# Eleven norm borders of a transformer stack: sums with one column of ones, and other places for sums, spreads and pieces

## The chip, the cores and the metric

The kernel runs as one program on one core of one Trainium2 chip. The metric is the device time of a run in microseconds (us). The five engines are TensorE (PE in the profile, PEld for its weight loads), VectorE (DVE), ScalarE (ACT), GpSimd (POOL) and SyncE (SP); they run side by side and wait for one another through semaphores.

## The reference, cut to what matters

The reference is a stack of four layers (differential attention, a gated linear recurrence, a sliding-window attention with sinks, differential attention again) followed by a second block (retention, a gated linear recurrent unit and a convolutional feed-forward), for 512 tokens of 1024 features in float32. The change touches only the norms between the parts:

```python
def layer_norm(x, g, b):
    mu = jnp.mean(x32, axis=-1, keepdims=True)
    var = jnp.mean(jnp.square(x32 - mu), axis=-1, keepdims=True)
    y = (x32 - mu) * lax.rsqrt(var + LN_EPS) * g.astype(jnp.float32) + b.astype(jnp.float32)
...
def rms_norm_2(x, w):
    y = x32 * lax.rsqrt(jnp.mean(x32 * x32, axis=-1, keepdims=True) + RMS_EPS)
...
        h = layer_norm(ALPHA * h + y, ln_g[i, 0], ln_b[i, 0])
        u = jnp.square(jax.nn.relu(h @ w_up[i])) @ w_down[i]
        h = layer_norm(ALPHA * h + u, ln_g[i, 1], ln_b[i, 1])
```

There are eight layer norms (numbered 0 to 7 here, even ones after a mixer, odd ones after a feed-forward) and three root-mean-square norms (8 to 10).

## The kernel before, in words

**Data.** Activations lie features-first: `h` is 128 partitions by 8 feature chunks by 512 tokens. Every big product is split into three float32r passes (high weight by high activation, high by low, low by high), so that each product of one weight block and one chunk is three matmuls (L472 to L474 over all 512 tokens, L571 to L573 over 256). Weights come as slabs of 1 MB through a ring of SBUF slots; GpSimd makes the high part of a slab (L451), VectorE the low part (L1637). A "unit" is what TensorE does with one slab: 8 chunks k = 0 to 7 of the contraction, two output blocks, results in two of the four PSUM banks `proj`. The other four banks are `mix`.

**A norm border.** The last two units ahead of a norm and the first two behind it are worked in halves of 256 tokens, so that the norm of one half lies under the matmuls of the other. The function `pair` writes TensorE's order by hand: first the first halves of both units, then the second halves, (ua, hf 0), (ub, hf 0), (ua, hf 1), (ub, hf 1), each of 8 chunks of 6 matmuls. A dictionary `points` says before which chunk two short jobs are put in:

- `stats(l, hf)` sums over the features: matmuls with the sums over chunks (`s1` of h, `s2` of its squares, 128x128 blocks) as weights and a tile of ones as the moving operand, 8 matmuls for a layer norm (16 instructions of the trace, since a float32 matmul is two passes), 4 for a root-mean-square norm.
- `spread(l, hf)` brings the two scalars of each token back along the free dimension (transposes of a broadcast column, L560).

A pair that produces the norm's input is called with `made=l` and holds stats and spread of half 0; the pair behind it is called with `read=l` and holds those of half 1. In the reading pair TensorE also waits before each chunk of half 0 for that chunk's low part, made by GpSimd at L446 (`half_x`, one semaphore step for each of five pieces: k = 0, k = 1, k = 2 and 3, k = 4 and 5, k = 6 and 7). At odd norms no pair follows: TensorE runs the four short units of the "ple" product (each 12 matmuls of 512 columns), with stats of half 1 behind the first and spread of half 1 behind the second, and then whole units that read the normalised values.

**VectorE at a border** (`border`) works strictly in its written order: add the product to h for half 0 and sum (`half`, `sums`, L1726 or L1728, L1743), the scalars of half 0 (`norm_scalars`, L1752 to L1765), `half(2, 1)` (which waits for the end of TensorE's unit ua), `apply(0, 0)` and `apply(0, 1)` (multiply and subtract for pieces 0 to 2 and 3 to 4 of half 0, L1777 and L1779), `sums(l, 2, 1)`, `half(3, 1)`, `sums(l, 3, 1)`, then the scalars and the applying of half 1. **ScalarE** squares (L1095), takes the square root (L1104), and for each piece writes the scaled value rounded (`xh`, L1112) and in full (`h`, L1115), in its own written order; GpSimd's L446 follows the latter. At odd norms ScalarE also copies the ple products out (L1414).

Of the kernel before, what the change touches and what calls it, by code (L numbers as in the profile page):

```python
# [21 lines left out]
ALU = mybir.AluOpType  # L22
ACT = mybir.ActivationFunctionType

P = 128
S = 512
D = 1024
# [4 lines left out]
RMS_EPS = 1e-6  # L32
# [178 lines left out]
def build(nc, stream, xin, pin, pos, vecs, relb, onehot, eye, swap, picks, decay, out):  # L211
    with ExitStack() as ctx:
# [255 lines left out]
        def _(pe):  # L468
# [71 lines left out]
            def stats(l, hf):  # L540

                for q, total, sem_ in ((0, s1, M("s1_added")), (1, s2, M("s2_added"))):
                    if q == 0 and l >= 2 * NL:
                        continue
                    pe.wait_ge(sem_, 5 * l + (5 if hf else 3))
                    for t in range(2 * hf, 2 * hf + 2):
                        for part in range(2):
                            at = (2 * q + t % 2) * P
                            last = nc.tensor.matmul(mix[:, 0, at:at + P], total[:, part, t * P:(t + 1) * P], ones[:, :],  # L549
                                                    start=part == 0, stop=part == 1, skip_group_check=True)  # L550
                last.then_inc(M("stats"), 1)

# [23 lines left out]
            def pair(ua, which, gen, made=None, read=None):  # L576

                ub = ua + 1
                points = {}
                if made is not None:  # L580
                    points[(ua, 1, 6 if made == 8 else 4)] = (stats, made, 0)
                    points[(ub, 1, 1) if made == 8 else (ua, 1, 7)] = (spread, made, 0)
                if read is not None:
                    points[(ub, 0, 1) if read == 8 else (ua, 0, 6)] = (stats, read, 1)
                    points[(ub, 0, 6 if read == 8 else 0)] = (spread, read, 1)
                for u, hf in ((ua, 0), (ub, 0), (ua, 1), (ub, 1)):
                    if hf == 0:
                        begin_unit(u)
                    for k in range(8):
                        if (u, hf, k) in points:  # L590
                            do, l, half = points[(u, hf, k)]
                            do(l, half)
                        if read is not None and hf == 0:
                            if read < 2 * NL:
                                pe.wait_ge(M("half_x"), 5 * read + PIECE_OF[k] + 1)
                            else:
                                pe.wait_ge(M("half_r"), 8 * (read - 8) + k + 1)
                        elif gen is not None:
                            operand_wait(which, gen, k)
                        last = half_chunk(u, k, hf, X if which == "x" else G, made is not None)  # L600
                    if hf:
                        last.then_inc(unit_done, 1)
                    elif made is not None:
                        last.then_inc(M("half_done"), 1)
# [436 lines left out]
        def _(act):  # L1041
# [64 lines left out]
            def ln_pieces(l, hf, pieces):  # L1106

                for p in pieces:
                    k0, n = PIECES[p]
                    act.wait_ge(M("ln_u"), 10 * l + 5 * hf + p + 1)  # L1110
                    for k in range(k0, k0 + n):
                        A(xh[:, k, cols(hf)], h[:, k, cols(hf)], ACT.Identity, scale=col("ln_g", 8 * l + k), bias=col("ln_b", 8 * l + k))\  # L1112
                            .then_inc(*own.sig(xh_ready if hf and k % 2 else None))
                    for k in range(k0, k0 + n):
                        A(h[:, k, cols(hf)], h[:, k, cols(hf)], ACT.Identity, scale=col("ln_g", 8 * l + k), bias=col("ln_b", 8 * l + k))\  # L1115
                            .then_inc(*own.sig(M("ln_full") if k == k0 + n - 1 else None))
# [260 lines left out]
            for layer in range(NL):  # L1377
                if layer % 3 == 0:
                    da_mixer(layer // 3, layer)
                elif layer == 1:  # L1380
                    hg_mixer(layer)
                else:
                    sw_mixer(layer)
                squares(2 * layer, 0)
                act.dma_start(pf[:, :, :], pin[layer]).then_inc(M("p_in"), 16)
                squares(2 * layer, 1)
                warm(ACT.Sqrt)
                squares(2 * layer, 2, 0)
                squares(2 * layer, 3, 0)
                std(2 * layer, 0)  # L1390
                squares(2 * layer, 2, 1)
                ln_pieces(2 * layer, 0, range(4))
                squares(2 * layer, 3, 1)
                ln_pieces(2 * layer, 0, (4,))
                std(2 * layer, 1)
                ln_pieces(2 * layer, 1, range(5))
                act.wait_ge(M("p_in"), 16 * (layer + 1))
                A(ph[:, :, :], pf[:, :, :], ACT.Copy).then_inc(*own.sig(M("p_hi")))
                ffn(layer)
                l = 2 * layer + 1  # L1400
                squares(l, 0)
                squares(l, 1)
                warm(ACT.Sqrt)
                squares(l, 2, 0)
                squares(l, 3, 0)
                std(l, 0)
                squares(l, 2, 1)
                ln_pieces(l, 0, range(3))
                squares(l, 3, 1)
                s0, u0 = PLAN.at[f"ple{layer}"]  # L1410

                def ple(j):
                    done(u0 + j)
                    A(po[:, 2 * j:2 * j + 2, :], banks(u0 + j), ACT.Copy).then_inc(*own.sig(rel["act"]))  # L1414

                ln_pieces(l, 0, (3,))
                ple(0)
                ln_pieces(l, 0, (4,))
                std(l, 1)
                ple(1)  # L1420
                ln_pieces(l, 1, (0, 1))
                ple(2)
                ln_pieces(l, 1, (2, 3))
                ple(3)
                ln_pieces(l, 1, (4,))
                s0, u0 = PLAN.at[f"gate{layer}"]
                for j in range(4 if layer < NL - 1 else 2):
                    done(u0 + j)
                    if j >= 2:
                        act.wait_ge(M("h_new"), layer * 4 + j - 1)  # L1430
                    A(sg[:, j % 2], banks(u0 + j), ACT.Sigmoid).then_inc(*own.sig(rel["act"]))
                    p2 = slice(2 * j, 2 * j + 2)
                    if layer < NL - 1:
                        act.wait_ge(M("h_new"), layer * 4 + j + 1)
                        A(gh[:, p2, :], h[:, p2, :], ACT.Copy).then_inc(*own.sig(gh_ready))
                    else:
                        squares(8, j)
# [179 lines left out]
        def _(dve):  # L1617
# [127 lines left out]
            def norm_scalars(l, hf):  # L1745

                c = 2 * hf
                m, v, r, mr = (small[:, a + c:a + c + 2] for a in (200, 204, 208, 212))
                total, squared = mix[:, 0, 0:2 * P:P], mix[:, 0, 2 * P:4 * P:P]
                dve.wait_ge(M("stats"), 2 * l + hf + 1)  # L1750
                if l < 2 * NL:
                    V.tensor_scalar(m, total, 1.0 / D, None, ALU.mult).then_inc(*own.sig())  # L1752
                    mine()
                    V.scalar_tensor_tensor(v, m, -1.0, m, ALU.mult, ALU.mult).then_inc(*own.sig())
                    mine()
                    V.scalar_tensor_tensor(v, squared, 1.0 / D, v, ALU.mult, ALU.add).then_inc(*own.sig())
                    mine()
                    V.tensor_scalar(v, v, 0.0, LN_EPS, ALU.max, ALU.add).then_inc(*own.sig(M("var_done")))
                else:
                    V.tensor_scalar(v, squared, 1.0 / D, RMS_EPS, ALU.mult, ALU.add).then_inc(*own.sig(M("var_done")))  # L1760
                dve.wait_ge(M("std_done"), 2 * l + hf + 1)
                V.reciprocal(r, v).then_inc(*own.sig(M("norm_ready") if l >= 2 * NL else None))
                if l < 2 * NL:
                    mine()
                    V.tensor_tensor(mr, m, r, ALU.mult).then_inc(*own.sig(M("norm_ready")))  # L1765
# [42 lines left out]
            def border(l, scaled, apply):  # L1808
# [21 lines left out]
                half(2, 1)  # L1830
                apply(0, 0)
                sums(l, 2, 1)
                if l % 2 == 0 or l > 8:
                    apply(0, 1)
                half(3, 1)
                sums(l, 3, 1)
                if l % 2 and l < 8:
                    apply(0, 1)
                norm_scalars(l, 1)
                apply(1, 0)  # L1840
                apply(1, 1)
# [655 lines left out]
```

## Time and profile before

| | |
|---|---|
| time, median of 3 runs | 3677.19 us (3676.24 to 3681.41) |
| profiled execution, its own time | 3681.41 us |
| its span | 3679.6 us |
| granted TensorE clock over the span | 0.989 |
| TensorE busy | 3565.8 us, 97% |
| VectorE, ScalarE, GpSimd busy | 1826.0, 941.3, 828.9 us |

The profile comes from one execution; it is the slowest of the three runs, 4.2 us over the median. Starts in a timeline are microseconds from the start of the span. A matmul's duration in a row includes its way through the array, so that rows of a dense stream overlap; the step from one start to the next is its cost.

### The profile page before, as it was taken

To read this page: it belongs to the slowest core of one execution; us is meant where nothing else is said; L and a number is where in the kernel's file an instruction comes from. 1 tells how busy PE (TensorE), PEld (TensorE's weight loads), DVE (VectorE), ACT (ScalarE), POOL (GpSimd) and SP (SyncE) were. 2 spreads that over 40 slices of the span, in tenths; PEclk is the share of its full clock that TensorE was granted. 3 is DMA by queue.
4 is the path that set the end of the run, shared out by engine and by line. 5 is a ranking of instruction groups with operands and counts; after the bars stand their busy time and mean duration, and the time that the engine had idled before them with its cause. 6 is when DMAs were issued, how large, how long until landed. Compare 5 with 4: busy or idle time off the path is not lost.

```text
span 3679.6 us, 44420 instructions
## 1 busy us (share of the span) xinstructions
PE 3565.8 (97%) x18618; PEld 2997.9 (81%) x18618; DVE 1826.0 (50%) x2281; ACT 941.3 (26%) x1662; POOL 828.9 (23%) x374
## 2 busy tenths in 40 slices
PE   8989999999999999999999998999989999999998
PEld 6778888798888888678888877888888887788887
DVE  5555334635563336564335555543464445563434
ACT  2552001312230013540113255210141214120102
POOL 2113222311032223122223211322221111222221
PEclk9999999999999999999999999999999999999999
DMA  5312222221122222222222321222212222222222
GB/s 201 103 58 92 92 103 81 93 78 60 56 89 92 100 95 92 72 75 92 94 101 81 109 81 58 95 92 102 82 69 92 81 92 79 94 103 92 103 92 69
DMA packets 57279, 329.58 MB, mean 90 GB/s; under 512 B 5579, under 2 KB 12235, under 8 KB 20348
## 3 DMA queue, kind: packets, MB, share of 16 engines
q1 hardware_dynamic: 44604, 303.79, 23.2%
q10 hardware_dynamic: 12480, 22.96, 1.9%
q8 instruction: 151, 2.47, 0.3%
q14 instruction: 44, 0.36, 0.0%
HBM read 323.96 MB, written 8.80 MB: 90 GB/s over the span
## 4 chain that ended last, share of the span: by engine, by line
PE 86%; DVE 8%; ACT 4%; issue 1%; POOL 1%; DMA 1%; DVEq 0%; ACTq 0%
PE proj L472 23%; PE proj L474 23%; PE proj L473 23%; PE proj L571 2%; PE proj L573 2%; PE proj L572 2%; DVE s L1743 2%; PE proj L505 2%; PE proj L507 1%; PE proj L506 1%; PE mix L738 1%; PE mix L644 1%; DVE wlo L1637 1%; PE mix L549 1%; PE mix L670 1%
## 5 line engine op out<-in xcount | busy, mean ns | idle before, releaser
L451 POOL TENSOR_SCALAR whi<-raw 128x2048 fp32r<-128x2048 f32 x286 | 729.0, 2549 | 2573.8 <-DMA raw<-in_stream 2573.8
L472 PE MATMUL proj<-gh,whi 128*128 128x512 f32 x1968 | 786.4, 400 | 14.7 <-DVE wlo L1643 10.6
L474 PE MATMUL proj<-gh,wlo 128*128 128x512 f32 x1968 | 771.4, 392 | 0.0
L473 PE MATMUL proj<-gl,whi 128*128 128x512 f32 x1968 | 770.9, 392 | 0.0
L1637 DVE TENSOR_TENSOR wlo<-raw,whi 128x2048 fp32r<-128x2048 f32 x286 | 700.0, 2450 | 126.6 <-POOL whi L451 114.9
L472 PE MATMUL proj<-xh,whi 128*128 128x512 f32 x1760 | 698.0, 397 | 14.9 <-DVE wlo L1637 5.8
L473 PE MATMUL proj<-xl,whi 128*128 128x512 f32 x1760 | 691.2, 393 | 0.0
L474 PE MATMUL proj<-xh,wlo 128*128 128x512 f32 x1760 | 691.1, 393 | 0.0
L472 PEld LDWEIGHTS proj<-gh,whi 128*128 128x128 f32 x1968 | 371.2, 189 | 108.3 <-issue 15.8
L474 PEld LDWEIGHTS proj<-gh,wlo 128*128 128x128 f32 x1968 | 371.0, 189 | 81.1
L473 PEld LDWEIGHTS proj<-gl,whi 128*128 128x128 f32 x1968 | 371.4, 189 | 79.2 <-issue 2.2
L472 PEld LDWEIGHTS proj<-xh,whi 128*128 128x128 f32 x1760 | 332.3, 189 | 95.1 <-issue 10.1
L474 PEld LDWEIGHTS proj<-xh,wlo 128*128 128x128 f32 x1760 | 332.6, 189 | 72.8
L473 PEld LDWEIGHTS proj<-xl,whi 128*128 128x128 f32 x1760 | 332.8, 189 | 71.8 <-issue 1.4
L1373 ACT ACTIVATE rl<-proj 128x1024 f32<-128x1024 f32 x64 | 65.7, 1027 | 946.8 <-PE proj L474 934.6
L1728 DVE TENSOR_TENSOR h<-h,proj 128x1024 f32<-128x1024 f32 (+1 forms) x76 | 80.0, 1053 | 350.8 <-PE proj L474 329.7
L2123 DVE SCALAR_TENSOR_TENSOR hid<-proj,rl 128x1024 f32<-128x1024 f32 x64 | 78.4, 1224 | 313.4 <-ACT rl L1373 312.5
L571 PE MATMUL proj<-xh,whi 128*128 128x256 f32 x640 | 184.5, 288 | 15.5 <-POOL xl L446 15.5
L572 PE MATMUL proj<-xl,whi 128*128 128x256 f32 x640 | 181.7, 284 | 0.0
L573 PE MATMUL proj<-xh,wlo 128*128 128x256 f32 x640 | 181.7, 284 | 0.0
L505 PE MATMUL proj<-whi,gh 128*128 128x256 f32 x512 | 152.1, 297 | 0.0
L506 PE MATMUL proj<-wlo,gh 128*128 128x256 f32 x512 | 145.8, 285 | 0.0
(295 smaller groups left out, 4331.5 us busy)
## 6 DMA issues: line engine op xcount, KB each, us to landing
raw<-in_stream SPq DMA_DIRECT2D x286, 1024.0 KB, 4.8
da_b<-bias_da ACTq DMA_DIRECT2D x16, 512.0 KB, 3.4
bias_da<-bias_rows ACTq DMA_DIRECT2D x8, 512.0 KB, 9.3
h<-in_x ACTq DMA_DIRECT2D x4, 512.0 KB, 8.7
bias_sw<-bias_table ACTq DMA_DIRECT2D x1, 2048.0 KB, 10.4
pf<-in_p ACTq DMA_DIRECT2D x4, 512.0 KB, 5.5
sw_b<-bias_sw ACTq DMA_DIRECT2D x4, 512.0 KB, 3.4
out_features<-fin SPq DMA_DIRECT2D x8, 256.0 KB, 2.3
```

Of the source, the lines that this page charges most:

```text
L451: nc.gpsimd.tensor_scalar(whi[SLOT[n]][:, :, :], raw[SLOT[n]][:, :, :], 1.0, 0.0, ALU.mult, ALU.add).then_inc(hi_done, 1)
L472: nc.tensor.matmul(out, wh, ah, start=first, stop=False, skip_group_check=check)
L473: nc.tensor.matmul(out, wh, al, start=False, stop=False, skip_group_check=check)
L474: return nc.tensor.matmul(out, wl, ah, start=False, stop=last, skip_group_check=check)
L505: nc.tensor.matmul(o, ah, wh, start=k == 0 and st % per == 0, stop=False, skip_group_check=True)
L506: nc.tensor.matmul(o, ah, wl, start=False, stop=False, skip_group_check=True)
L571: nc.tensor.matmul(o, wh, ah, start=k == 0 and (j if own_banks else hf) == 0, stop=False, skip_group_check=True)
L572: nc.tensor.matmul(o, wh, al, start=False, stop=False, skip_group_check=True)
L573: last = nc.tensor.matmul(o, wl, ah, start=False, stop=k == 7, skip_group_check=True)
L1637: V.tensor_tensor(wlo[SLOT[n]][:, :, :], raw[SLOT[n]][:, :, :], whi[SLOT[n]][:, :, :].bitcast(F32), ALU.subtract).then_inc(*own.sig(split_ ...
L1728: ins = V.tensor_tensor(o, o, y, ALU.add)
L2123: V.scalar_tensor_tensor(hid[:, :, :], banks(u), 0.0, rl[:, :, :], ALU.max, ALU.mult).then_inc(*own.sig(rel["dve"]))
```

## The change

The sums use one column of ones instead of 128, and write to one column for each token block (columns 0 to 3 the sums, 4 to 7 the sums of squares). The points move: stats of half 1 from before chunk 6 to before chunk 4 of (ua, hf 0) of the reading pair (not at norm 8); spread of half 0 from before chunk 7 of (ua, hf 1) to before chunk 0 of (ub, hf 1) of the producing pair (at norm 8 from chunk 1 to chunk 2 of (ub, hf 1)). ScalarE does all five pieces of half 0 before it squares the last pair of chunks of half 1, at all eight layer norms. VectorE does `apply(0, 1)` before `half(3, 1)` at norms 1, 3, 5 and 7 too, as it did at the others.

```diff
-                            at = (2 * q + t % 2) * P
-                            last = nc.tensor.matmul(mix[:, 0, at:at + P], total[:, part, t * P:(t + 1) * P], ones[:, :],
+                            last = nc.tensor.matmul(mix[:, 0, 4 * q + t:4 * q + t + 1], total[:, part, t * P:(t + 1) * P], ones[:, 0:1],
...
-                    points[(ub, 1, 1) if made == 8 else (ua, 1, 7)] = (spread, made, 0)
+                    points[(ub, 1, 2 if made == 8 else 0)] = (spread, made, 0)
                 if read is not None:
-                    points[(ub, 0, 1) if read == 8 else (ua, 0, 6)] = (stats, read, 1)
+                    points[(ub, 0, 1) if read == 8 else (ua, 0, 4)] = (stats, read, 1)
...
                 squares(2 * layer, 2, 1)
-                ln_pieces(2 * layer, 0, range(4))
+                ln_pieces(2 * layer, 0, range(5))
                 squares(2 * layer, 3, 1)
-                ln_pieces(2 * layer, 0, (4,))
                 std(2 * layer, 1)
...
                 squares(l, 2, 1)
-                ln_pieces(l, 0, range(3))
+                ln_pieces(l, 0, range(5))
                 squares(l, 3, 1)
...
-                ln_pieces(l, 0, (3,))
                 ple(0)
-                ln_pieces(l, 0, (4,))
                 std(l, 1)
...
                 sums(l, 2, 1)
-                if l % 2 == 0 or l > 8:
-                    apply(0, 1)
+                apply(0, 1)
                 half(3, 1)
                 sums(l, 3, 1)
-                if l % 2 and l < 8:
-                    apply(0, 1)
                 norm_scalars(l, 1)
```

VectorE's reads of the sums follow the new columns (`mix[:, 0, c:c + 2]` and `mix[:, 0, 4 + c:6 + c]` for the strided `total` and `squared`); they stay 128x2.

## Rows read from the trace of the kernel before

**Rows 1.** The page: TensorE's busy time, share of the span, instructions.
```profile
PE 3565.8 (97%) x18618; PEld 2997.9 (81%) x18618; DVE 1826.0 (50%) x2281; ACT 941.3 (26%) x1662; POOL 828.9 (23%) x374
```

**Rows 2.** Groups by line: busy us, mean ns, idle before and its releasers.
```profile
L549 PE MATMUL mix<-ones,s 128*128 128x128 f32 x304 | 41.5, 291 | 9.9 <-DVE s L1743 9.8
L560 PE MATMUL mix<-ident,small 128*128 128x128 f32 x76 | 14.0, 307 | 17.9 <-DVE small L1765 16.9 <-DVE small L1762 0.7
```

**Rows 3.** Timeline of TensorE at norm 0: start, duration, [idle before and releaser].
```profile
274.54 2.05 PE L549 MATMUL mix<-ones,s 128*128 128x128 f32 x16 [0.18 <-DVE s L1743]
278.58 0.60 PE L560 MATMUL mix<-ident,small 128*128 128x128 f32 x4
...
290.90 0.39 PE L571 MATMUL proj<-xh,whi 128*128 128x256 f32 x1 [1.73 <-POOL xl L446]
...
297.52 0.62 PE L560 MATMUL mix<-ident,small 128*128 128x128 f32 x4
...
308.32 0.36 PE L571 MATMUL proj<-xh,whi 128*128 128x256 f32 x1 [1.55 <-POOL xl L446]
```

**Rows 4.** Timeline of VectorE at norm 0.
```profile
279.93 0.69 DVE L1726 SCALAR_TENSOR_TENSOR h<-h,proj 128x512 f32<-128x512 f32 x1 [1.92 <-PE proj L573]
...
288.94 0.69 DVE L1726 SCALAR_TENSOR_TENSOR h<-h,proj 128x512 f32<-128x512 f32 x1
289.66 1.74 DVE L1743 TENSOR_TENSOR s<-s,h 128x512 f32<-128x512 f32 x1
291.50 0.69 DVE L1743 TENSOR_TENSOR s<-s,sq 128x512 f32<-128x512 f32 x1
```

**Rows 5.** Timelines of ScalarE and GpSimd at norm 0.
```profile
289.66 0.63 ACT L1095 ACTIVATE sq<-h 128x512 f32<-128x512 f32 x1 [0.15 <-DVE h L1726]
290.20 1.08 ACT L1112 ACTIVATE xh<-h,vec 128x256 fp32r<-128x256 f32 x2
...
289.58 1.26 POOL L446 TENSOR_TENSOR xl<-h,xh 128x512 fp32r<-128x512 f32 x1 [2.16 <-ACT h L1115]
```

**Rows 6.** Timelines of TensorE and VectorE at norm 1, in order of time.
```profile
649.74 0.69 DVE L1728 TENSOR_TENSOR h<-h,proj 128x512 f32<-128x512 f32 x1
...
651.81 2.05 PE L549 MATMUL mix<-ones,s 128*128 128x128 f32 x16
...
652.65 0.69 DVE L1777 TENSOR_TENSOR h<-h,mix 128x512 f32<-128x512 f32 x1
...
660.46 1.11 PE L560 MATMUL mix<-ident,small 128*128 128x128 f32 x4 [3.84 <-DVE small L1765]
...
671.29 0.47 PE L472 MATMUL proj<-xh,whi 128*128 128x512 f32 x1 [0.37 <-POOL xl L446]
```

**Rows 7.** Timelines of TensorE and its weight loads, float32 with few columns, and L549.
```profile
27.52 0.29 PEld L615 LDWEIGHTS mix<-small,ones 64*128 64x128 f32 x2 [1.98 <-issue]
...
771.07 1.89 PE L738 MATMUL mix<-hg_q,hg_k 128*128 128x64 f32 x16
...
2749.50 1.78 PEld L549 LDWEIGHTS mix<-ones,s 128*128 128x128 f32 x8 [2.94 <-DVE s L1743]
```

**Rows 8.** Windows: length, busy us of PE, PEld, DVE, ACT, POOL, then PEclk.
```profile
28.80:31.90 3.10, 3.10 (x10) 2.36 (x9) 2.86 (x13) 0.15 (x1) 1.73 (x1) 0.51 0.99 163
...
291.70:295.10 3.40, 3.40 (x18) 3.40 (x17) 0.49 (x1) 0.56 (x2) 2.76 (x2) 0.50 0.00 0
660.40:663.60 3.20, 3.14 (x10) 2.65 (x11) 1.86 (x6) 1.08 (x3) 1.85 (x1) 0.50 0.03 5
```

**Rows 9.** Timeline of TensorE at norm 4.
```profile
1625.96 0.39 PE L571 MATMUL proj<-xh,whi 128*128 128x256 f32 x1 [1.77 <-POOL xl L446]
...
1631.71 0.62 PE L560 MATMUL mix<-ident,small 128*128 128x128 f32 x4 [0.92 <-DVE small L1765]
```

**Rows 10.** Timelines at norm 8 (VectorE) and norm 9 (TensorE).
```profile
2735.30 0.87 DVE L1803 TENSOR_TENSOR tln<-h,mix 128x256 f32<-128x256 f32 x2 [1.75 <-PE mix L560]
...
3271.01 1.63 PE L549 MATMUL mix<-ones,s 128*128 128x128 f32 x8 [3.13 <-DVE s L1743]
```

More of the change, by code:

```diff
@@ L1748, in norm_scalars @@
                 m, v, r, mr = (small[:, a + c:a + c + 2] for a in (200, 204, 208, 212))
-                total, squared = mix[:, 0, 0:2 * P:P], mix[:, 0, 2 * P:4 * P:P]
                 dve.wait_ge(M("stats"), 2 * l + hf + 1)
                 if l < 2 * NL:
-                    V.tensor_scalar(m, total, 1.0 / D, None, ALU.mult).then_inc(*own.sig())
+                    V.tensor_scalar(m, mix[:, 0, c:c + 2], 1.0 / D, None, ALU.mult).then_inc(*own.sig())
                     mine()
@@ L1755, in norm_scalars @@
                     mine()
-                    V.scalar_tensor_tensor(v, squared, 1.0 / D, v, ALU.mult, ALU.add).then_inc(*own.sig())
+                    V.scalar_tensor_tensor(v, mix[:, 0, 4 + c:6 + c], 1.0 / D, v, ALU.mult, ALU.add).then_inc(*own.sig())
                     mine()
@@ L1759, in norm_scalars @@
                 else:
-                    V.tensor_scalar(v, squared, 1.0 / D, RMS_EPS, ALU.mult, ALU.add).then_inc(*own.sig(M("var_done")))
+                    V.tensor_scalar(v, mix[:, 0, 4 + c:6 + c], 1.0 / D, RMS_EPS, ALU.mult, ALU.add).then_inc(*own.sig(M("var_done")))
                 dve.wait_ge(M("std_done"), 2 * l + hf + 1)
```

## The prediction, made before the changed kernel was run

> **What bounds the kernel now.** I read the page first: TensorE is busy for 97% of the span [rows 1], so a microsecond counts if it makes TensorE wait or gives it more to do, and VectorE, ScalarE and GpSimd count only where TensorE waits for them. Then the groups by line: all 304 stats instructions are busy for 41.5 us, and TensorE sat idle for 17.9 us ahead of spreads, almost all of it for VectorE's scalars [rows 2]. These are the sizes to be had. Last the timelines of three borders, because only they show which wait ends last. At norm 0 TensorE waits 1.73 us for piece 3 of the low parts and goes on at 290.90, does chunks 4 and 5, the sums of half 1, chunks 6 and 7 and the spread at 297.52, and then runs into a wait of 1.55 us at 308.32 for a piece that follows from that spread [rows 3]. So the time of the second spread carries through to the end of the border, and what comes before it is what the change moves.
>
> **Part 1, one column.** From a stats start at 274.54 to the spread at 278.58 lie 16 passes and 3 chunks; with 1.87 us for the passes (2.05 less the tail of one, about 0.2) a chunk costs 0.72 us [rows 3]. A pass of 128 columns thus costs 0.117 us. What is a pass of one column? Not shown; the nearest rows: 16 passes of 64 columns take 1.89 us with the tail, 0.108 each; the two weight loads of a product with four columns take 0.29 us together with one of about 0.19, so they follow at 0.10 [rows 7]. The weights are 128x128 as before, and the load sets the pace. I take 0.108: 0.15 us less for each of the 16 layer-norm stats, half for the six others. Bounds: nothing saved, or all 1.9 us saved at each (37 us in all, 22 halves, six of them short), which the rows with 4 and 64 columns exclude as far as they go. At half clock the loads of 8 passes take 1.78 us, 0.207 each [rows 7], so a one-column stats then costs 3.3 us.
>
> The Trainium skill ("TensorE: Matmul & The Clock Gate", section "Back-to-back issue gap") gives about 25 ns between matmuls of 1 to 64 columns; by that figure 16 passes would take an estimated 0.4 us and stats would save 1.5 us each. Its section on LDWEIGHTS there gives the columns of the weights over 1.2 GHz, 107 ns, and this trace's 0.10 to 0.108 us agrees with the second; the 0.207 us at half clock are longer than it says.
>
> **Part 2, the spread of half 0, one chunk later.** At norm 0 VectorE waits 1.92 us for the end of unit ua before `half(2, 1)` at 279.93 [rows 4]. The spread (0.44 us of four transposes, 0.60 with its tail [rows 3]) now lies behind that end, and the stats is 0.15 us shorter, so `half(2, 1)` starts 0.6 us earlier; the spread is ready when it ends. VectorE then works without a gap to the second sums, so that whole chain gains 0.6 us. At norms 9 and 10, with half as many transposes, it gains 0.3. At norm 8 VectorE waits 1.75 us for the spread itself [rows 10], and one chunk later is 0.65 us lost.
>
> **Part 3, even layer norms: the sums of half 1 before chunk 4.** They need the last sum of squares. Before, it ended at 291.50 + 0.69 = 292.2 [rows 4], ahead of TensorE's arrival at chunk 6. Now ScalarE does piece 4 ahead of the square: at 290.20 this piece began, two instructions in 1.08 us and two more of the same kind, about 2.0 in all, and the square takes 0.63 [rows 5]. Shifted: piece 4 from 288.9 to 290.9, square to 291.5, sum to 292.2 if it takes 0.69. It will lie beside GpSimd's subtraction of piece 4, and the sum that lay beside such a one took 1.74 [rows 4, 5]. I take 292.6. So TensorE goes on at 292.6 and not at 290.90, and chunks 4 and 5, which lay under this wait, come after it. The left work until the spread: stats and four chunks, 1.75 + 2.88 = 4.65 at full clock, about 6.3 with the slow stretch that rows 8 show after such waits (two in 3.4 us of half clock). Spread at 298.9 for 297.5: +1.4. Norm 2 shows the same pattern as norm 0; norms 4 and 6 ran at full clock and reached the spread at 1631.71, 5.75 us after going on at 1625.96 [rows 9]. There it becomes 1.7 later plus 6.3: +2.3. Four borders: +7.4. If the clock stays up: 4.65 for 6.3, and together +1. VectorE's order stays as it was here.
>
> **Part 4, norms 1, 3, 5, 7.** Here nothing waited at the sums (651.81), but the spread waited 3.84 us [rows 6], since ScalarE took pieces and a copy ahead of the root. Now `apply(0, 1)`, four operations of 0.72 from 652.65, goes ahead of `half(3, 1)` and its sums, which took from 649.74 to 652.65 [rows 6]. Pieces 3 and 4 become ready 2.9 + 0.6 us earlier, piece 3 at 652.65 + 1.44 - 3.5 = 650.6; ScalarE works on both until 654.6, squares to 655.3, and the sum ends between 656.0 and 657.0 (0.69 or 1.74, rows 4). I take 656.6. TensorE is there at 651.8 and waits 4.8 us. Then stats at half clock 3.3, one ple unit 2.8: spread at 662.8 for 660.46, +2.3. Given back: the slow stretch of 3.2 us after the old wait [rows 8] now lies before the spread and no longer stretches what follows (1.6 us, of which ScalarE's and GpSimd's chain to 671.29 lets about 1.4 through). +0.9 each, +3.6 for four. Queued behind the waiting stats: the ple unit, whose banks are free.
>
> **Part 5, norm 9.** Stats already waited 3.13 us for its sum, until 3271.01 [rows 10]. Two chunks less lie under the wait: 2 x 0.72 more after it, 0.3 less from part 2, 0.1 from part 1: +1.1. Norm 8 +0.65 (part 2), norm 10 -0.4, for the chain to the end is VectorE's.
>
> **The clock.** The granted clock was 0.50, which is 1.2 of 2.4 GHz, for 3.4 and 3.2 us after TensorE had waited at norms 0 and 1 [rows 8], and in both stretches it then streamed many columns. A stats of one column streams 2 columns for each block where it streamed 256. Near the start the clock fell to 0.51 after a wait and a product of four columns [rows 7, 8]. If such a stats counts for the clock as a wait, the slow stretch after each of the eight long waits goes on for another one (1.6 us each, 13 in all), and the eight first-half stats may bring on stretches of their own (half of them, 6 us). If it counts as work, nothing. Between 0 and 19 I take 8, since the nearest row, with four columns, is a case of a fall but also had a wait.
>
> The Trainium skill's same page, "PE-mode transpose", says that transposes do not count as busy in the same way for the clock; it speaks for the upper end, and no row here tells it from the wait beside it.
>
> **Sum.** +7.4 + 3.6 + 0.65 + 1.1 - 0.4 = +12.35, with the clock +20. Against the profiled 3681.4 that is 3701.4; the median lies 4.2 lower, so 3697.
>
> **Rivals.**
> - *Clock untouched (a)*: part 3 and 4 as above, one column counts as work: +12, 3689. The slow stretches of before are all explained by waits, which speaks for it.
> - *Clock at its worst (b)*: 12 + 19 and the sums 0.5 later in eight borders: +35, 3712. For it: the row of four columns.
> - *Hidden (c)*: the clock does not fall after the longer waits. Then part 3 gives +1 and part 4 reaches the ScalarE chain first, 0.6 less than before at each, -2.4: with the rest about 0, 3677. Against it: after 3.84 us of waiting it fell [rows 6, 8].
> - *Faster (d)*: the weight load does not set the pace of a one-column pass, and the stats nearly vanish. All 37 us of part 1 go instead of the 3 counted, each on TensorE's own path: +12 - 34 = -22, 3655, with the clock untouched. It decides from a pass under about 0.07 us, where the gain outgrows the 15 us of the moves; the loads at 0.10 beside four columns [rows 7] speak against it. The Trainium skill's gap for few columns, above, is this rival's rule.
> - *No effect of the moves* cannot be: the order is written out by hand and no planner stands between.
>
> **How the numbers follow.** What a measurement of this kernel can tell from no change is 0.2%, 7.4 us. Forecast (+8 to +27) 0.55, (a) as low as +7.4 0.17, (b) 0.14, (c) 0.10, (d) 0.04. Slower 0.86, same 0.10, faster 0.04. The range leaves out the faster half of (c), (d) and the tail of (b): 3682 to 3712.
>
> **What would show it.** In the changed kernel: L549 at about 0.108 us a pass at full clock (0.02 would be rival d); at even norms L549 with an idle time of 3 to 4 us ahead for VectorE's sum of squares, and the L571 wait before chunk 4 gone; at odd norms the idle time moved from L560 to L549, 4 to 5 us; L549 at norm 9 idle for over 4; `half(2, 1)` 0.6 us nearer to the first stats; a mean clock below 0.989. The forecast is wrong if VectorE's sum of squares ends before TensorE is at chunk 4, or if the second spread follows the first by no more than before (18.9 us at norm 0, from 278.58 to 297.52).

## The result, and the profile after

| | before | changed |
|---|---|---|
| median | 3679.3 us (4 runs, 3676.24 to 3681.76) | 3702.06 us (4 runs, 3701.27 to 3708.82) |
| profiled execution, span | 3681.41, 3679.6 us | 3699.42, 3697.6 us |
| mean granted TensorE clock | 0.989 | 0.984 |

Ratio 1.0066, 95% interval 1.0049 to 1.0084: 23 to 24 us slower, where 3697 us (20 us slower) was forecast and 3682 to 3712 given. The median before is that of the runs beside it, 2 us over that of the three runs ahead of the prediction.

The groups by line of the changed kernel answer to [rows 2] (L548 is the old L549, L559 the old L560, L570 to L572 the old L571 to L573):

```profile
L548 PE MATMUL mix<-ones,s 128*128 128x1 f32 x304 | 46.5, 278 | 37.6 <-DVE s L1739 37.4
L559 PE MATMUL mix<-ident,small 128*128 128x128 f32 x76 | 12.8, 286 | 0.7 <-DVE small L1757 0.7
L570 PE MATMUL proj<-xh,whi 128*128 128x256 f32 x640 | 190.5, 298 | 6.5 <-POOL xl L446 6.5
```

The idle time has moved from the spreads and from GpSimd's pieces to the sums, as foretold, and it has hardly grown: 9.9 + 17.9 us before L549 and L560 before, with 15.5 before the half-width matmuls, are 43.3; now 37.6 + 0.7 + 6.5 = 44.8. So waiting does not explain 23 us. What grew is TensorE's busy time, from 3565.8 us [rows 1] to 3584.1, and these 18.3 us are as much as the 18.0 by which the two profiled spans differ:

```profile
PE 3584.1 (97%) x18618; PEld 3017.3 (82%) x18618; DVE 1830.7 (50%) x2281; ACT 941.0 (25%) x1662; POOL 829.3 (22%) x374
```

The sums, of 1/128 of the width, are busy for 46.5 us and not 41.5, and the unchanged matmuls of L570 for 190.5 and not 184.5.

TensorE's timeline at norm 0 shows why; it answers to [rows 3]:

```profile
270.58 1.95 PE L548 MATMUL mix<-ones,s 128*128 128x1 f32 x16 [0.17 <-DVE s L1739]
276.84 0.60 PE L559 MATMUL mix<-ident,small 128*128 128x128 f32 x4
...
288.56 1.05 PE L548 MATMUL mix<-ones,s 128*128 128x1 f32 x8 [2.26 <-DVE s L1739]
290.53 1.87 PE L548 MATMUL mix<-ones,s 128*128 128x1 f32 x8 [0.92 <-DVE s L1739]
297.07 0.60 PE L559 MATMUL mix<-ident,small 128*128 128x128 f32 x4
307.85 0.36 PE L570 MATMUL proj<-xh,whi 128*128 128x256 f32 x1 [1.55 <-POOL xl L446]
```

From the first sums to the first spread lie 6.26 us for 16 passes and four chunks, where 4.65 were expected, and nothing waits in between (0.17 us ahead of the sums is all). The windows of that stretch, with the granted clock behind the five busy times:

```profile
268.40:270.40 2.00, 2.00 (x17) 1.81 (x16) 1.86 (x3) 0.56 (x1) 0.00 (x0) 1.00 0.00 0
270.40:272.30 1.90, 1.73 (x17) 1.72 (x16) 0.82 (x2) 0.07 (x1) 0.00 (x0) 1.00 0.00 0
272.30:276.10 3.80, 3.80 (x21) 3.80 (x21) 0.98 (x6) 0.20 (x1) 0.00 (x0) 0.55 0.00 0
276.10:277.00 0.90, 0.90 (x10) 0.90 (x9) 0.00 (x0) 0.00 (x0) 0.00 (x0) 1.00 0.00 0
```

TensorE's busy time has no gap to speak of, yet right behind the one-column sums the granted clock falls: 0.55 is the mean of 3.8 us, most of it at the lower of the two levels, 0.50. Norms 2, 6 and 8 show the same (6.23, 5.87 and 5.28 us where 4.65 and 3.8 would be full speed); norms 1, 3, 4, 5, 7, 9 and 10 do not. Behind the second sums it is the rule:

```profile
290.50:292.40 1.90, 1.87 (x9) 1.88 (x9) 0.00 (x0) 0.00 (x0) 1.73 (x1) 0.50 0.00 0
292.40:297.10 4.70, 4.70 (x25) 4.70 (x26) 0.98 (x6) 0.20 (x1) 0.00 (x0) 0.57 0.00 0
297.10:300.00 2.90, 2.90 (x27) 2.90 (x26) 2.16 (x5) 1.38 (x3) 0.21 (x1) 1.00 0.00 0
```

At norm 1, which answers to [rows 6], the wait stands before the sums and is gone before the spread:

```profile
654.29 1.37 PE L548 MATMUL mix<-ones,s 128*128 128x1 f32 x8 [2.91 <-DVE s L1739]
656.26 1.87 PE L548 MATMUL mix<-ones,s 128*128 128x1 f32 x8 [0.60 <-DVE s L1739]
662.54 0.60 PE L559 MATMUL mix<-ident,small 128*128 128x128 f32 x4
```

**An account by borders.** From TensorE's timelines I took for each norm the time from the first matmul of its producing pair to the first matmul that follows the border and reads the next part's operand. Norm 7 is taken to the start of norm 8's pair, since the two borders overlap. The feed-forward bodies between take the same time in all kernels (285.0 us); the mixers do not quite (from norm 1 to norm 2 295.5 us before, 297.0 changed, 293.9 with the spread alone moved), and the start differs by up to 4 us (259.9 us to the first border before, 256.0 after). So the differences of the borders are cleaner than those of the spans, but they are single traces: at norm 8, in the five runs whose edit does not touch it, they are -0.1 to -1.6 us.

| difference to before, us | norms 0, 2, 4, 6 | 1, 3, 5, 7 | 8 | 9 | 10 | sum |
|---|---|---|---|---|---|---|
| forecast, waits | +7.4 | +3.6 | +0.65 | +1.1 | -0.4 | +12.35, clock +8 |
| changed kernel | +13.6 | +1.9 | +3.3 | +3.0 | -0.3 | +21.5 |
| with 128 columns back | +1.4 | +0.5 | -1.0 | +1.2 | +0.5 | +2.6 |

With the start (-3.9) and the mixers (+0.5) the 21.5 us make the 18.0 between the two spans.

### The profile page after: what moved, and what is told of

Read it like the earlier page. It is cut to its first block, busy times and chain, and to the rows that moved or that the text cites. A ratio compares the mean times of both kernels' runs of the same rounds, so it can differ in the third digit from the quotient of the medians.

```text
span 3697.6 us, 44420 instructions
## 1 busy us (share of the span) xinstructions
PE 3584.1 (97%) x18618; PEld 3017.3 (82%) x18618; DVE 1830.7 (50%) x2281; ACT 941.0 (25%) x1662; POOL 829.3 (22%) x374
## 4 chain that ended last, share of the span: by engine, by line
PE 87%; DVE 7%; ACT 4%; issue 1%; DMA 0%; POOL 0%; ACTq 0%; DVEq 0%
PE proj L472 23%; PE proj L474 23%; PE proj L473 23%; PE proj L570 2%; PE proj L571 2%; PE proj L572 2%; DVE s L1739 2%; PE proj L505 2%; PE proj L507 2%; PE proj L506 2%; PE mix L737 1%; PE mix L643 1%; DVE wlo L1633 1%; PE mix L548 1%; PE mix L669 1%
## 5 line engine op out<-in xcount | busy, mean ns | idle before, releaser
L570 PE MATMUL proj<-xh,whi 128*128 128x256 f32 x640 | 190.5, 298 | 6.5 <-POOL xl L446 6.5
L571 PE MATMUL proj<-xl,whi 128*128 128x256 f32 x640 | 187.8, 293 | 0.0
L572 PE MATMUL proj<-xh,wlo 128*128 128x256 f32 x640 | 187.6, 293 | 0.0
L446 POOL TENSOR_TENSOR xl<-h,xh 128x512 fp32r<-128x512 f32 (+1 forms) x80 | 95.8, 1200 | 232.2 <-ACT h L1114 232.2
## 6 DMA issues: line engine op xcount, KB each, us to landing
out_features<-fin SPq DMA_DIRECT2D x8, 256.0 KB, 2.3
```

Of the source, the lines that this page charges most:

```text
L446: nc.gpsimd.tensor_tensor(xl[:, k:k + n, cols(hf)], h[:, k:k + n, cols(hf)], xh[:, k:k + n, cols(hf)].bitcast(F32), ALU.subtract)\
L570: nc.tensor.matmul(o, wh, ah, start=k == 0 and (j if own_banks else hf) == 0, stop=False, skip_group_check=True)
L571: nc.tensor.matmul(o, wh, al, start=False, stop=False, skip_group_check=True)
L572: last = nc.tensor.matmul(o, wl, ah, start=False, stop=k == 7, skip_group_check=True)
```

## The experiments

My theory after the result: the moves cost little, and the width costs most of the 23 us through TensorE's clock. The rival, my own forecast: the waits cost 12, the clock 8.

**One column alone.** The kernel before, with only this:

```diff
-   ... matmul(mix[:, 0, at:at + P], total[...], ones[:, :],
+   ... matmul(mix[:, 0, at:at + 1], total[...], ones[:, 0:1],
```

> Only the width of the sums is changed (1 column of ones instead of 128, same places). If a one-column sum counts as idleness for the clock: faster by 0.15 us at each stats, but stretches at 1.2 GHz behind some first-half sums, where nothing waits (as the changed kernel has at norms 0, 2, 6 and 8), and longer ones behind second-half sums; in all +5 to +12 us over the kernel before, mean clock under 0.989. If it counts as work: 22 stats, -2 to -3 us, clock as before.

Measured: 1.0017 (1.0008 to 1.0026), medians 3686.43 against 3677.28, clock 0.987. Slower, though it takes work away: the first of the two expectations holds, at 6 to 9 us. By the borders 6.7 us lie at the four even norms, 3.7 at norm 4 alone. At norms 0 and 2 the slow stretch behind the first sums stands for one that the kernel before had at the second sums, so that these borders grow by only 0.7 and 0.8; the longer stretches expected behind second sums show, of the even norms, at norm 4 only. At norm 4, where nothing waits before the first sums, the timeline and the windows of this kernel are

```profile
1611.05 1.95 PE L549 MATMUL mix<-ones,s 128*128 128x1 f32 x16
1616.47 0.73 PE L560 MATMUL mix<-ident,small 128*128 128x128 f32 x4
```

```profile
1611.00:1613.00 2.00, 1.95 (x17) 1.95 (x18) 0.69 (x1) 0.00 (x0) 0.00 (x0) 1.00 0.00 0
1613.00:1616.50 3.50, 3.50 (x19) 3.50 (x20) 0.98 (x6) 0.20 (x1) 0.00 (x0) 0.54 0.00 0
```

5.42 us for what took 4.04 before, and the border is 3.7 us longer.

**128 columns back in the changed kernel.** All moves kept, sums at their old width and places.

> The changed kernel with 128 columns back (and their old places), all moves kept. If the moves make the waits and the width only the clock: +8 to +14 us over the kernel before, 9 to 15 under the changed one, no slow stretch behind first-half sums. If the width did nothing: the changed kernel's time plus 3, about +25 us.

Measured: 1.0009 (1.0000 to 1.0017), 3680.77 us. The moves together cost about 3 us, where 8 to 14 were expected; the other 19 to 21 come with the width (and with the places in PSUM, which go back with it: one column alone, at the old places, is slower too). By the records of the granted clock the trace before lies at the lower level for about 80 us in all, the changed kernel for 121, this one for 85. In its windows the stretch behind the first sums of norm 0 stays at full clock, and behind the second ones the clock is back 3.5 us after they began (VectorE's sum of the squares stands first):

```profile
288.04 1.34 DVE L1740 TENSOR_TENSOR s<-s,sq 128x512 f32<-128x512 f32 x1 [0.64 <-ACT sq L1095]
287.46 3.67 PE L549 MATMUL mix<-ones,s 128*128 128x128 f32 x16 [2.26 <-DVE s L1740]
293.84 0.60 PE L560 MATMUL mix<-ident,small 128*128 128x128 f32 x4
```

```profile
270.80:273.00 2.20, 2.04 (x19) 2.02 (x19) 0.81 (x2) 0.06 (x1) 0.00 (x0) 1.00 0.00 0
273.00:276.50 3.50, 3.50 (x32) 3.50 (x31) 1.53 (x7) 0.20 (x1) 0.00 (x0) 1.00 0.00 0
287.40:291.00 3.60, 3.54 (x17) 3.34 (x18) 1.35 (x2) 0.60 (x2) 3.44 (x2) 0.56 0.00 0
291.00:293.80 2.80, 2.80 (x26) 2.80 (x25) 0.97 (x6) 0.20 (x1) 0.14 (x1) 1.00 0.00 0
```

**64 columns in the changed kernel.** `at:at + 64` and `ones[:, 0:64]`, at the old places.

> The changed kernel with 64 columns in the sums, all moves kept. A pass of 64 columns should last as long as one of 1 column (0.108 us, the weight load), so only what streams through the array differs. If the clock answers to the streamed columns, the first-half sums bring on no slow stretch, or few, and the time lies near that with 128 columns: +2 to +8 us over the kernel before. If it was the length of a pass or the places of the sums in PSUM: as the changed kernel, +20 to +25.

Measured: 1.0039 (1.0027 to 1.0052), 3691.85 us, +14. My expectation missed the size: 64 columns are not nearly as good as 128 but lie halfway between (+3, +14, +24 us). The duration of the sums is nearly that with one column (2.00 us for 1.95), as the timeline of norm 0 shows:

```profile
273.50 2.00 PE L549 MATMUL mix<-ones,s 128*128 128x64 f32 x16 [0.17 <-DVE s L1740]
278.26 0.60 PE L560 MATMUL mix<-ident,small 128*128 128x128 f32 x4
...
289.98 1.38 PE L549 MATMUL mix<-ones,s 128*128 128x64 f32 x8 [2.26 <-DVE s L1740]
291.95 1.97 PE L549 MATMUL mix<-ones,s 128*128 128x64 f32 x8 [0.60 <-DVE s L1740]
```

So the length of a pass does not explain the time, nor do the places in PSUM, which one column alone left as they were. What is left is the number of columns that stream (with what is read and written for them, which these runs do not tell apart). The first sums here brought on no slow stretch at any norm (4.76 us to the spread at norm 0), the second ones did.

**One column in the first or in the second halves only.** The changed kernel with `n = 1 if hf == 0 else 128` columns, and the reverse.

> The changed kernel with one column in the sums of half 0 only, 128 in those of half 1. With 128 everywhere it was 3.3 us over the kernel before, with 1 everywhere about 24. By the borders of the changed kernel, slow stretches behind first-half sums came at norms 0, 2, 6 and 8 and cost about 1.6 to 2.2 each: +8 to +12 over the kernel before. If the clock answers to sums only when there is a wait beside them: +3, as with 128.

> The changed kernel with one column in the sums of half 1 only, 128 in those of half 0. These lie behind a wait of 3 to 4 us. If a one-column sum lengthens the wait for the clock, nearly every border has a full slow stretch or two behind it: +12 to +17 over the kernel before, the larger part of the 20 us that the width costs. If the long wait alone decides: +3, as with 128.

Measured: 1.0034 (1.0022 to 1.0046), 3689.25 us, and 1.0032 (1.0019 to 1.0044), 3688.57 us; +12.4 and +11.7 by the medians. The first is at the upper end of what was expected, the second just under what was expected of it. Less the 3.3 of the moves, the halves cost about 9 and 8 us, together 17 to 18 of the 19 to 21. The first halves cost as much as the second, which I had not expected. A reading, not tested by itself: a slow stretch behind first sums takes work from full speed, for with 128 columns nothing is slow there, while at the second sums 128 columns have a slow stretch too, part of which falls on the wait.

**Sums of half 1 before chunk 4, alone.**

```diff
-   points[(ub, 0, 1) if read == 8 else (ua, 0, 6)] = (stats, read, 1)
+   points[(ub, 0, 1) if read == 8 else (ua, 0, 4)] = (stats, read, 1)
```

> Only the sums of half 1 go from before chunk 6 to before chunk 4 (norms 0, 2, 4, 6, 9). If the place exposes a wait for VectorE's last sum of squares: about 1.3 us at norms 0 to 6 and 1.4 at norm 9, +6 to +9 us in all, with an idle time of 3 us ahead of L549. If the sums are ready by then or the wait is hidden: within 1 us of the kernel before.

Measured: 1.0010 (1.0001 to 1.0018), 3680.49 us, 3 to 4 us slower, between the two expectations; by borders +0.5 at norms 0 to 6 together, +1.4 at norm 9, +0.9 at norm 10, which the edit does not touch. The wait is there, 2.28 us at norm 0, but it replaces the one of 1.73 for GpSimd's piece:

```profile
285.12 0.39 PE L571 MATMUL proj<-xh,whi 128*128 128x256 f32 x1 [0.70 <-POOL xl L446]
289.09 2.05 PE L549 MATMUL mix<-ones,s 128*128 128x128 f32 x16 [2.28 <-DVE s L1743]
294.30 0.62 PE L560 MATMUL mix<-ident,small 128*128 128x128 f32 x4 [0.30 <-DVE small L1765]
```

The sums end the wait when their first operand, the sum of h, is there; their first eight passes run while ScalarE and VectorE still make the squares' sum. I expected a wait for the last sum of squares.

**The spread of half 0 one chunk later, alone.**

> Only the spread of half 0 goes one chunk later. By the forecast VectorE's next addition comes 0.45 us earlier at norms 0 to 7 and 0.2 at 9 and 10, and norm 8 loses 0.65: -2 to -4 us. The rival, that the spread's result is what VectorE needs, gives +0.7 us at each, up to +7.

Measured: 0.9987 (0.9978 to 0.9996), 3671.58 us, 5 to 6 us faster, more than the 2 to 4 expected. By borders norm 8 lost 0.6, as worked out, though that is within the scatter of that border. So I left that one where it was:

```diff
-   points[(ub, 1, 1) if made == 8 else (ua, 1, 7)] = (spread, made, 0)
+   points[(ub, 1, 1 if made == 8 else 0)] = (spread, made, 0)
```

> The spread of half 0 one chunk later at all norms but 8. With the spread moved at all norms the time fell by 5 to 6 us, and norm 8 was the one that lost (0.6 us by its border). So a little under that one: -5 to -7 us against the kernel before, faster than both kernels. If the gain was only the chance of where slow stretches fall, it is not reproduced: 0 to -3.

Measured: 0.9979 (0.9970 to 0.9988), 3670.01 us against 3677.32: 7 to 8 us faster than the kernel before, a little over the expectation, and 32 faster than the changed one. VectorE's timeline, to be read against [rows 4], has the addition 277.42 - 272.46 = 4.96 us after TensorE's first sums, where it was 279.93 - 274.54 = 5.39, and the idle time ahead of it is 1.49 for 1.92:

```profile
277.42 0.69 DVE L1726 SCALAR_TENSOR_TENSOR h<-h,proj 128x512 f32<-128x512 f32 x1 [1.49 <-PE proj L573]
```

**The orders, alone.** For norms 1, 3, 5 and 7 the lines of `border` and of ScalarE's second half as in the change; for the even ones `ln_pieces(2 * layer, 0, range(5))` before `squares(2 * layer, 3, 1)`.

> Only norms 1, 3, 5 and 7: VectorE applies pieces 3 and 4 and ScalarE finishes all five pieces before the last square; 128 columns, old places. The forecast was +0.9 us at each, +3.6; the borders of the changed kernel with 128 columns back showed +0.4 in sum over these four, with the spread one chunk later inside. If that gained 0.6 at each by itself, this edit costs it back: +2 to +4. Rival, the order is free because the wait only moves from the spread to the sums: within 1 us. In both, the idle time of 3.8 us ahead of L560 moves to L549.

> Only ScalarE's order at norms 0, 2, 4 and 6 (piece 4 before the last square); sums before chunk 6 as before. The last sum of squares should end about 0.5 to 1.7 us later than before, 292.7 to 293.9 instead of 292.2 at norm 0, and TensorE arrives at chunk 6 at 293.0 (norm 0) or 1.5 us after it goes on (norm 4). If this wait is new: +0.5 to +1 us at each, +2 to +4 in all. If it is covered: within 1 us.

Measured: 1.0000 (0.9991 to 1.0009), 3677.99 us, and 0.9997 (0.9988 to 1.0006), 3676.18 us: neither can be told from nothing; the two expectations of a loss (+2 to +4 each) did not come true, their rivals did. The odd order moves the wait to the sums and about keeps its length, as the timeline of norm 1 shows against [rows 6] (3.35 + 0.82 us for 3.84):

```profile
651.92 1.16 PE L549 MATMUL mix<-ones,s 128*128 128x128 f32 x8 [3.35 <-DVE s L1741]
653.90 2.08 PE L549 MATMUL mix<-ones,s 128*128 128x128 f32 x8 [0.82 <-DVE s L1741]
659.15 0.60 PE L560 MATMUL mix<-ident,small 128*128 128x128 f32 x4
```

**The orders with the later spread.** 128 columns, sums before chunk 6.

> The orders of VectorE and ScalarE of the changed kernel and the later spread (not at norm 8), but sums of 128 columns and those of half 1 before chunk 6: what is left if the two costly parts are undone. The orders alone measured 0 (odd norms) and -1 (even norms), the spread alone -7.7. If they add: -7 to -10. If the later sum of squares at even norms and the spread get in each other's way: -4 to -6, no better than the spread alone.

Measured: 0.9986 (0.9977 to 0.9994), 3672.95 us. That is 4 to 5 us faster, the second of the two expectations: the orders give nothing on top of the spread. The spread alone, except at norm 8, is the best version found, but the difference between the two is no larger than their intervals allow for chance.

## Why the prediction was right in its sum and wrong in its terms

- **Part 1, the price of a pass**: held. 16 passes take 1.95 us with the tail for 2.05, about 0.11 us each, and eight at half clock 1.87. A pass of one column costs about what one of 64 costs, so rival d (nearly vanishing sums) is out. (The bound of 37 us should read 36, 19 times 1.9; only rival d uses it.)
- **Part 2, the spread later**: the 0.44 us for the spread alone held (5.39 to 4.96), and so, within the scatter of that border, did the loss at norm 8. In the changed kernel itself the gain cannot be seen, for the slow stretch lies in front of it: there the addition at norm 0 comes 6.5 us after the sums. I gave it as a small term inside others; alone it is worth 5 to 8 us. The borders of the run without norm 8 show where: -0.4 us at norms 0, 4 and 6, the 0.44 of the forecast; -0.9 at norms 1, 3 and 7, where in the trace before the four transposes behind the wait ran at half clock (1.11 us at norm 1) and here do not (0.65); -1.3 at norm 2 and -0.1 at norm 5. Norm 8, which it leaves alone, is 1.6 us shorter as well, so some of the difference of these two traces is chance.
- **Part 3, even norms, +7.4**: the step that failed. "The left work until the spread: stats and four chunks" is wrong by half the stats, which run under the wait for the squares' sum. The wait itself ended as forecast: with 128 columns back that sum ends at 288.04 + 1.34 = 289.38 in a trace whose first border starts 3.5 us earlier (256.4 for 259.9), so at 292.9 for 292.6; but the spread follows it by 4.5 us, at 293.84, and not by 6.3. For the slow stretch that I put behind the wait lies, with 128 columns, over the wait's end and the passes (287.4 to 291.0 at norm 0), so that the chunks behind run at full clock. In all, +1.4 for the four with the width undone, +0.5 with the sums' place alone.
- **Part 4, odd norms, +0.9 each**: the times were right (sums go on at 656.3, spread at 662.5, against 656.6 and 662.8 forecast), but in the changed kernel it comes to +1.9 for the four, not +3.6, and with 128 columns to +0.5. So most of what this term did cost is clock too.
- **Part 5**: norm 9, +1.1, held: +1.2 with 128 columns and +1.4 with the move alone; in the changed kernel, with the clock, +3.0.
- **The clock, +8 between 0 and 19**: the mis-sized term. It is 19 to 21 us by the runs with 1 and with 128 columns, at or over the upper end I gave, and the waits' term is 3 and not 12. That the two errors nearly cancel is luck. The reading behind the upper end was the right one, that behind a one-column sum the clock can fall as it does behind a wait: mean clock 0.989 to 0.984 is 0.005 of 3690 us, 18 us.
- **Rivals**: (a), the width as plain work, is refuted by one column alone being slower. (b), the clock at its worst, has the right mechanism and too large a sum, for it stood on the same 12. (c) was half right: the moves do cost little, but not because the clock stays up.

## What to carry to other kernels

Cutting TensorE work that lies in a dense stream can cost time: here 16 passes with one column for 128 gained 0.1 us of 2.05, and the matmuls behind them could run at half clock for most of the next 3.8 us. Price a wait from what the waiting job needs first and what it can do meanwhile, not from its last operand alone, and look what already waits in the place where the wait will go. Small jobs put into a hand-written order are best judged one by one: here one of five edits was worth 7 us and was buried under another that cost 20.

## What the runs showed of the hardware that was not expected

The granted clock fell to 0.50 behind 1.95 us of one-column float32 passes with TensorE busy throughout (at norm 4 of the kernel with one column alone, 1.95 of 2.00 us busy and no idle time ahead). With 128 columns the first sums never brought it on: in none of the nine traces with 128 columns there, eleven norms each, and not in the one with 64.

It did not come everywhere either. In the three traces with one column in the first sums (the changed kernel, one column alone, one column in the first halves only) it came at 13 of the 15 borders of norms 0, 2, 4, 6 and 8, and at none of the 18 of the other norms, though the sums of the odd norms are the same 16 passes. What tells the two kinds apart was not looked for, so a count of few-column jobs does not give the price.

The cost goes by degree: with all moves made, +3, +14 and +24 us at 128, 64 and 1 columns, with the duration of 16 passes all but equal (2.05, 2.00 and 1.95 us). The Trainium skill ("TensorE: Matmul & The Clock Gate", "PE-mode transpose") says of transposes that they do not count as busy in the same way. No run here tests that of transposes; what these runs show is a fall behind float32 passes of few columns.
